# Second layer's recurrence: head norm and state scaling on ScalarE in pieces, substitution rows behind the state

## What is computed

```python
a = jax.nn.sigmoid(a0 + (xa @ a1) @ a2)
kk = (k * k_k).reshape(B, S, H, N)
kk = kk / jnp.maximum(jnp.linalg.norm(kk, axis=-1, keepdims=True), 1e-12)
def step(state, inp):
    r_t, w_t, k_t, v_t, kk_t, a_t = inp
    sk = jnp.einsum('bhvk,bhk->bhv', state, kk_t)
    state = state * w_t[:, :, None, :] - sk[..., None] * (kk_t * a_t)[:, :, None, :] + v_t[..., None] * k_t[:, :, None, :]
    return state, jnp.einsum('bhvk,bhk->bhv', state, r_t)
y = head_norm(y, LNX_EPS) * lnx_g + lnx_b          # per token and head: (y - mean) / sqrt(var + eps)
bonus = jnp.sum(rh * kh * r_k, axis=-1, keepdims=True) * vh
out = einsum('bsf,fd->bsd', (y + bonus) * jax.nn.silu(g), w_out)
```

## Time and profile before

| | us |
|---|---|
| median of 3 runs | 4260.09 (4253.25 to 4288.84) |
| the profiled execution | 4255.36 |
| its span, first to last instruction | 4253.6 |
| TensorE matmuls busy | 3758.1 (88%) |
| VectorE busy | 2016.2 (47%) |
| ScalarE busy | 1703.1 (40%) |
| mean granted TensorE clock | 0.91 of 2.4 GHz |

### The profile page before, as it was taken

How to read it: one execution, slowest core, us unless ns; L and a number is a source line. 1 busy time by engine, 2 the same in 40 slices (tenths; PEclk the granted TensorE clock), 3 DMA queues, 4 the chain that set the end, 5 groups by cost and what they waited for, 6 DMA issues and landing times. The chain is left out here.

```text
span 4253.6 us, 48223 instructions
## 1 busy us (share of the span) xinstructions
PE 3758.1 (88%) x18866; PEld 3044.6 (72%) x18866; DVE 2016.2 (47%) x3934; ACT 1703.1 (40%) x3132; POOL 107.6 (3%) x120
## 2 busy tenths in 40 slices
PE   6999679889995999999788999999788999998789
PEld 5888337668883777777666777777676688877666
DVE  3143323354335667775334455555544355565441
ACT  3222461344332333342234444444433465655420
POOL 0011120000000000000000000000000000000000
PEclk9999799989995777788899999999898999999789
DMA  3333302212222121121321111010122111110310
GB/s 125 114 127 114 111 0 80 85 45 94 103 76 74 40 63 40 40 50 40 124 79 41 33 31 31 26 36 21 45 90 80 63 32 40 35 35 11 134 50 40
DMA packets 219642, 265.62 MB, mean 62 GB/s; under 512 B 62620, under 2 KB 142612, under 8 KB 218392
## 3 DMA queue, kind: packets, MB, share of 16 engines
q1 hardware_dynamic: 219416, 262.53, 18.9%
HBM read 191.95 MB, written 70.52 MB: 62 GB/s over the span
## 5 line engine op out<-in xcount | busy, mean ns | idle before, releaser
L320 PE MATMUL bank<-wh,XH 128*128 128x512 f32 x1344 | 556.1, 414 | 55.9 <-DVE wl L304 38.2
L320 PE MATMUL bank<-wh,XL 128*128 128x512 f32 x1344 | 530.3, 395 | 0.0
L320 PE MATMUL bank<-wl,XH 128*128 128x512 f32 x1344 | 530.0, 394 | 0.0
L2325 PE MATMUL bank<-XH,wh 128*128 128x512 f32 x1040 | 427.2, 411 | 32.1 <-DVE wl L2314 19.8
L2325 PE MATMUL bank<-XH,wl 128*128 128x512 f32 x1040 | 411.5, 396 | 0.0
L2325 PE MATMUL bank<-XL,wh 128*128 128x512 f32 x1040 | 410.7, 395 | 0.0
L320 PEld LDWEIGHTS bank<-wh,XH 128*128 128x128 f32 x1344 | 257.0, 191 | 126.0 <-issue 50.7
L304 DVE TENSOR_TENSOR wl<-raw,wh 128x1024 fp32r<-128x1024 f32 x128 | 155.6, 1235 | 312.8 <-ACT wh L295 311.6
L320 PEld LDWEIGHTS bank<-wh,XL 128*128 128x128 f32 x1344 | 257.4, 192 | 60.4 <-issue 10.0
L320 PEld LDWEIGHTS bank<-wl,XH 128*128 128x128 f32 x1344 | 256.5, 191 | 56.1
L320 PE MATMUL bank<-XH,wh 128*128 128x512 f32 x704 | 278.7, 396 | 5.9 <-DVE XL L1435 5.9
(11 more groups left out here) (401 smaller groups left out, 7367.2 us busy)
## 6 DMA issues: line engine op xcount, KB each, us to landing
sc_zt<-stage SPq DMA_DIRECT2D x88, 256.0 KB, 2.0
raw<-in_att_w_in SPq DMA_DIRECT2D x33, 512.0 KB, 4.2
raw<-in_even_w_in SPq DMA_DIRECT2D x32, 512.0 KB, 5.1
raw<-in_odd_w_in SPq DMA_DIRECT2D x32, 512.0 KB, 4.7
raw<-in_rec_w_in SPq DMA_DIRECT2D x32, 512.0 KB, 4.0
sc_h<-H SPq DMA_DIRECT2D x24, 512.0 KB, 2.6
H<-sc_h SPq DMA_DIRECT2D x24, 512.0 KB, 7.8
sc_z<-stage SPq DMA_DIRECT2D x40, 256.0 KB, 2.0
```

Of the source, the lines that this page charges most:

```text
L320: done = e.matmul(out, lhsT, rhs, start=k == 0 and j == 0, stop=k == NK - 1 and j == 2)
L2325: done = e.matmul(bank[:, :], x[:, k, :], y[:, k, ts], start=k == 0 and j == 0, stop=k == NK - 1 and j == 2)
```

## The change

- **Tail.** Eleven parts instead of six, over four chunks instead of two (and over chunks 0 to 3 of the next pair for the second half, which shares its rule with the first). ScalarE copies the whole bank into `yc` (part 0), VectorE sums it from there (1). ScalarE squares each head's 64 columns with the negative mean as bias and with an accumulator output, four heads in part 2 and four in part 3; VectorE makes the variance of the eight sums (4); the root is ScalarE's (5); VectorE makes the reciprocal and `shift` = negative mean x reciprocal, both 128 x 8 (6); ScalarE scales each head's 64 columns with a scale and a bias from pointers (7 and 8, four heads each); transposes (9); gain, bonus, bias, gate and the store (10). The load of the next `g` stands behind it, in chunk 3. `bv` gets a third buffer.
- **State.** `SG` is made by ScalarE right behind `R`, instead of by VectorE.
- **Substitution.** Instead of three rows at each place of chunks 2 to 5 there are two at the first, two at the second and five at the third, behind the new state.
- **Norm of the keys.** ScalarE's two passes over k come out of `scan` as `squares`, one chunk earlier (chunk 2). The norm's matmuls are split in three (`norms`, in chunks 3 to 5, three, three and two of them) and go to the free last columns of bank 4, whose first part the scores use; root, floor and reciprocal move from chunk 4's last place to chunk 5's second.

The diff, cut to its core (renames of flags, buffers and the list of shared banks are left out):

```diff
@@ -1541,11 +1541,11 @@
-    some(0, "load", "values", "gates", ("lora", 0), ("lora", 1), "scan", "norm", "spread", "centre", "unit", "key", "exps", "be", "al")
+    some(0, "load", "values", "gates", ("lora", 0), "squares", ("lora", 1), "scan", ("norms", 0, 8), "norm", "spread", "centre", "unit", "key", "exps", "be", "al")
     some(0, *[("alike", m) for m in range(4)], ("pack", 0), "ka", "rh", "rkr")
...
     some(0, ("pack", 1), "bonus")
-    ahead = {0: ["scan"], 8: ["norm"], 11: ["spread", "centre"], 16: ["unit"], 21: ["key", "exps"], 27: ["be", "ka"]}
+    ahead = {0: ["squares", "scan"], 8: [("norms", 0, 8), "norm"], 11: ["spread", "centre"], 16: ["unit"], 21: ["key", "exps"], 27: ["be", "ka"]}
     for s in range(NSUB):
...
@@ -1557,8 +1557,10 @@
         group = groups[u // 2 + 1] if u < 62 else None
-        if n == 4:
-            order.append(("tail", p, 0, 0))
+        last = (p - 1, 1) if n < 4 else (p, 0)
+        tail = [TAILS.get(3 * (n % 4) + part, ()) if last[0] >= 0 else () for part in range(3)]
+        if n % 4 == 0 and last[0] >= 0:
+            order.append(("tail", *last, 0))
         order.append(("chain", p, n, "r"))
...
@@ -1566,72 +1568,65 @@
             some(p + 1, "rh", ("alike", 1))
-            if p:
-                order.append(("tail", p - 1, 1, 0))
         elif n == 1:
...
             some(p + 2, "be", "al")
+        order += [("tail", *last, part) for part in tail[0]]
         some(p + 1, *[("solve", s) for s in solved(n, 0)])
         order.append(("chain", p, n, "u"))
+        if 3 <= n <= 5:
+            some(p + 2, ("norms", 3 * n - 9, min(3 * n - 6, 8)))
         if after:
...
             order.append(("level", *group, "F" if n % 2 else "X"))
-        if n == 0:
-            if p:
-                order.append(("tail", p - 1, 1, 1))
-        elif n == 1:
+        if n == 1:
             some(p + 1, ("pack", 0))
-            if p:
-                order.append(("tail", p - 1, 1, 3))
-        elif n == 4:
-            order.append(("tail", p, 0, 1))
         elif n == 5:
-            order.append(("tail", p, 0, 3))
+            some(p + 2, "norm")
         elif n == 6:
...
             some(p + 2, "ka")
-            order.append(("tail", p, 0, 5))
+        order += [("tail", *last, part) for part in tail[1]]
         some(p + 1, *[("solve", s) for s in solved(n, 1)])
...
             order.append(("level", *group, "G"))
+        order += [("tail", *last, part) for part in tail[2]]
         if n == 0:
             some(p + 1, ("alike", 2), "rkr")
-            if p:
-                order.append(("tail", p - 1, 1, 2))
         elif n == 1:
-            if p:
-                order += [("tail", p - 1, 1, 4), ("tail", p - 1, 1, 5), ("gates", p)]
             some(p + 1, ("pack", 1), "bonus")
...
         elif n == 2:
-            some(p + 2, ("lora", 0))
+            some(p + 2, ("lora", 0), "squares")
         elif n == 3:
             some(p + 2, ("lora", 1), "scan")
-        elif n == 4:
-            some(p + 2, "norm")
-            order.append(("tail", p, 0, 2))
         elif n == 5:
...
             some(p + 2, "spread", "centre")
-        elif n == 6:
-            order.append(("tail", p, 0, 4))
         elif n == 7:
             some(p + 2, "values", ("alike", 0))
+        if n == 3 and p:
+            order.append(("gates", p))
         some(p + 1, *[("solve", s) for s in solved(n, 2)])
-    order += [("tail", 7, 1, part) for part in range(6)]
+    order += [("tail", 7, 1, part) for part in range(11)]
     return order
...
-    at = 3 * (3 * (n - 2) + part)
-    return range(at, min(at + 3, NSUB)) if 2 <= n <= 5 else ()
+    at = 9 * (n - 2) + (0, 2, 4)[part]
+    return range(at, min(at + (2, 2, 5)[part], NSUB)) if 2 <= n <= 5 else ()
+TAILS = {0: (1,), 2: (2,), 3: (3,), 4: (4,), 6: (5,), 7: (6,), 8: (7,), 9: (8,), 10: (9,), 11: (10,)}
...
@@ -1846,15 +1841,19 @@
                     .then_inc(*self.lor.up(p, rest[0], h))
-        elif what == "norm":
-            key = (what, p)
+        elif what == "norms":
+            first, end = rest
             e.wait_ge(*self.scaled.at("squares", p))
...
                 e.wait_ge(*self.tables.at("heads2"))
-            wait_all(e, self.bank_free(key))
-            for n in range(NS):
-                done = e.matmul(self.bank(*key)[:, 2 * n:2 * n + 2], self.t[:, self.chunk(n)], self.cols2[:, :], start=True, stop=True)
-            done.then_inc(*self.side.up(what, p))
+            if p >= 2:
+                e.wait_ge(*self.masked.at(p - 2, 3 + first // 3, 0))
+            elif p == 1:
+                e.wait_ge(*self.root.at(0))
+            for n in range(first, end):
+                done = e.matmul(self.c.banks[4][:, 3 * P + 2 * n:3 * P + 2 * n + 2], self.t[:, self.chunk(n)], self.cols2[:, :],
+                                start=True, stop=True)
+            done.then_inc(*self.side.up("norm", p, end))
         elif what == "unit":
...
@@ -1910,6 +1909,10 @@
             e.wait_ge(*self.fact.at("rh", p))
+            if p == 0:
+                e.wait_ge(*self.root.at(1))
+        if n == NS - 1 and p + 2 < 8:
+            e.wait_ge(*self.root.at(p + 2))
         for hh in range(2):
...
@@ -1948,7 +1951,7 @@
             if n % 4 == 0 and u:
-                e.wait_ge(*self.tail.at("free", *((p, 0) if n else (p - 1, 1))))
+                e.wait_ge(*self.tailed.at("free", *((p, 0) if n else (p - 1, 1))))
             for hh in range(2):
...
@@ -2011,8 +2007,10 @@
         elif what == "norm":
-            e.wait_ge(*self.side.at(what, p))
-            e.activation(self.nr[:, :], self.bank(what, p)[:, 0:2 * NS], ACT.Sqrt).then_inc(*self.root.up(p))
+            e.wait_ge(*self.side.at(what, p, NS))
+            if p >= 2:
+                e.wait_ge(*self.masked.at(p - 2, 6, 0))
+            e.activation(self.nr[:, :], self.c.banks[4][:, 3 * P:3 * P + 2 * NS], ACT.Sqrt).then_inc(*self.root.up(p))
         elif what == "spread":
...
@@ -2060,8 +2058,35 @@
             e.activation(self.R[:, :], bank[:, 0:P], ACT.Copy).then_inc(*self.rucopy.up(part, p, n))
+            if 0 < n < NS - 1:
+                e.wait_ge(*self.state.at(p, n - 1))
+                e.activation(self.SG[:, :], self.S[(NS * p + n) % 2][:, :], ACT.Copy, scale=self.G[p % 3][:, n:n + 1]) \
+                    .then_inc(*self.old.up(p, n))
         else:
...
+    def ac_tail(self, e, p, half, part):
+        m, v, mr, yc = self.sums[half], self.vars[half], self.shift[half], self.yc
+        group = lambda j: slice(64 * j, 64 * j + 64)
+        if part == 0:
+            e.wait_ge(*self.step.at("y", p, 4 * half + 3))
+            before = (p, 0) if half else (p - 1, 1)
+            if before[0] >= 0:
+                e.wait_ge(*self.yturned.at(*before))
+            e.activation(yc[:, :], self.c.banks[7][:, :], ACT.Copy).then_inc(*self.tailed.up("free", p, half))
+        elif part in (2, 3):
+            e.wait_ge(*self.tail.at("mean", p, half))
+            for j in range(4 * part - 8, 4 * part - 4):
+                done = e.activation(self.sq[:, group(j)], yc[:, group(j)], ACT.Square, bias=m[:, j:j + 1], accum_out=v[:, j:j + 1])
+            done.then_inc(*self.tailed.up("squares", p, half, part))
+        elif part == 5:
+            e.wait_ge(*self.tail.at("var", p, half))
+            e.activation(v[:, :], v[:, :], ACT.Sqrt).then_inc(*self.tailed.up("root", p, half))
+        elif part in (7, 8):
+            e.wait_ge(*self.tail.at("shift", p, half))
+            for j in range(4 * part - 28, 4 * part - 24):
+                done = e.activation(yc[:, group(j)], yc[:, group(j)], ACT.Identity, scale=v[:, j:j + 1], bias=mr[:, j:j + 1])
+            done.then_inc(*(self.tailed.up("scaled", p, half) if part == 7 else self.tailed.up("normed", p, half)))
...
@@ -2188,16 +2213,13 @@
             return
-        if part == "u" and n:
-            e.wait_ge(*self.state.at(p, n - 1))
-            e.tensor_scalar(self.SG[:, :], self.S[u % 2][:, :], G, None, ALU.mult).then_inc(*self.state.up("old", p, n))
-        elif part == "y":
+        if part == "y":
             if u == 0:
...
             else:
-                e.wait_ge(*self.state.at("old", p, n))
+                e.wait_ge(*self.old.at(p, n))
             e.wait_ge(*self.step.at("s", p, n))
...
@@ -2209,32 +2231,27 @@
     def ve_tail(self, e, p, half, part):
-        y8 = lambda t: t.rearrange("p (a f) -> p a f", a=8)
-        m, v, yc, sq, zo = self.sums[half], self.vars[half], self.yc[:, :], self.sq[:, :], self.zo[half][:, :]
-        bank, each = self.c.banks[7][:, :], [P, 8, 64]
-        if part == 0:
-            e.wait_ge(*self.step.at("y", p, 4 * half + 3))
-            e.tensor_reduce(m[:, :], y8(bank), AX, ALU.add, negate=True).then_inc(*self.tail.up("sum", p, half))
+        m, v, zo = self.sums[half], self.vars[half], self.zo[half][:, :]
+        if part == 1:
+            e.wait_ge(*self.tailed.at("free", p, half))
```

(18 more changed lines are left out.)

33 lines of the change are left out of this document (13 added, 20 removed).

## The result

| | before | changed |
|---|---|---|
| median of 11 runs each, us | 4266.98 (4247.24 to 4288.84) | 4304.91 (4298.66 to 4309.55) |
| ratio to before | | 1.0083 (95%: 1.0066 to 1.0101) |
| the profiled execution, us | 4255.36 | 4301.42 |
| one period of pairs 1 to 5, us | 87.2 | 92.8 |
| of it TensorE idle / busy, us | 6.2 / 81.0 | 7.6 / 85.2 |

A forecast was written before the change was run, and what follows sets the result against it. TensorE's order was taken to bound the stage, at a reduced clock, with VectorE close behind. Six periods at -0.7 us mechanical and -2.2 clock, -2.5 at the start and +4.5 at the end gave -15.4: 4243 us, range 4212 to 4280.

The forecast's parts named there:

- the sum: Second layer's recurrence: six periods at -0.7 us mechanical and -2.2 clock, start -2.5, end +4.5, together -15.4 us.

The follow-up runs named there:

- e2: Kernel before with the tail's new places and ScalarE's copy, squares and scalings; state scaling, substitution rows and keys' norm as before: 4275.8 us, ratio 1.0015.
- e5: Changed kernel with unused identity products added in TensorE's waits, 12 in n=3 and 10 in n=7: 4279.4 us, ratio 1.0036 to before.
- e11: e5 with the first half's two products of alike 0 made twice, in the wait for zo in n=7: 4266.3 us, ratio 0.9998 to before.

## What to carry to other kernels

Ask of each chunk which engine times it before costing a move: work on TensorE that is free in a chunk that VectorE times has its full price, and at the slow clock, one chunk on. Where TensorE runs close to full, cost a new wait by what follows it as well: two waits of 1.2 to 1.3 us were each followed by 10 to 24 us at half clock here (another of 1.2, in the kernel before, by 3.4 at most), and 2.3 us of waits behind elementwise groups lengthened a period by 5.4 (e2). And look at the DMA queue first: taking a store and a load from ahead of one critical load, with the work that issues them, was worth 0.8% by itself, more than any other part of the change. Last, cost the first and last periods too: 13.5 of the 46 us were lost in one that the sum had left out.

## Not expected of the hardware

Products whose results nobody reads made the kernel faster: 132 in e5 took it from a ratio of 1.0083 to 1.0036, and with the doubled ones of e11 it came to 0.9998. Behind a wait of 1.32 us, TensorE was busy for 23.63 of the next 23.90 us and ran at a mean clock of 0.51; a full queue of small fp32 products did not bring 2.4 GHz back in that time. Behind a wait of 1.19 us elsewhere the clock stayed full for the next 12.2 us. An accumulator read of 0.19 us behind a pass of 0.33 costs no time of its own (squares and scalings both start 0.34 us apart).
